# The SSD pipeline of a decoder layer: carried state multiplied by unscaled C on the full array, skip term by a diagonal on the tensor engine, sample state turned

## What is computed

```python
def step(h, inp):                       # once per chunk, h is the carried state
    xc, dtc, Bc, Cc = inp
    acs = jnp.cumsum(dtc * Ar, axis=1)
    decay = jnp.exp(jnp.where(tril, acs[:, :, None] - acs[:, None, :], -jnp.inf))
    xdt = xc * dtc[..., None]
    cb = jnp.einsum('blgn,bsgn->blsg', Cc, Bc)
    y_diag = jnp.einsum('blsg,blsgr,bsgrp->blgrp', cb, decay, xdt)
    y_off = jnp.einsum('blgn,bgrpn,blgr->blgrp', Cc, h, jnp.exp(acs))
    to_end = jnp.exp(acs[:, -1:] - acs)
    h_new = jnp.exp(acs[:, -1])[..., None, None] * h + jnp.einsum('bsgn,bsgr,bsgrp->bgrpn', Bc, to_end, xdt)
    return h_new, y_diag + y_off
...
y = y + d_skip[:, None] * xs            # then the gate silu(z), a norm per group and a gain
```

## Time and profile before

| | us |
|---|---|
| median of 3 runs | 4075.02 (4072.28 to 4075.45) |
| the profiled execution | 4073.7 |
| its span in the profile | 4071.9 |
| first and last instruction of the stage `sg` | 2017.9 to 2324.2 |
| PE, DVE, ACT, POOL busy over the whole span | 3724.5, 1986.9, 943.4, 358.0 |

### The profile page before, as it was taken

The page is one execution under the profiler, slowest core; times in us unless marked ns, Lnnn a source line. Parts: engine busy times, 40 slices in busy tenths (PEclk is TensorE's granted clock), DMA queues, the critical chain, the costliest instruction groups (busy, mean ns, idle before and its releaser), DMA issues. The chain is left out here.

```text
span 4071.9 us, 48044 instructions
## 1 busy us (share of the span) xinstructions
PE 3724.5 (91%) x18116; PEld 2942.2 (72%) x18116; DVE 1986.9 (49%) x4404; ACT 943.4 (23%) x2079; POOL 358.0 (9%) x372
## 2 busy tenths in 40 slices
PE   5999999998996999999777589789899999999997
PEld 3888888885654888888655456445467888888886
DVE  3444444442123888764299732244441354453544
ACT  2111111112131222221377400156300221111111
POOL 0000000000000000000055411354100000000000
PEclk8999999998998999999888699899989999999999
DMA  4333343215441132222367332200114022222222
GB/s 182 121 124 124 117 153 124 103 66 192 115 110 68 53 104 84 83 84 83 101 221 221 114 108 81 71 16 11 60 49 152 11 93 83 83 94 77 90 83 83
DMA packets 178142, 406.45 MB, mean 100 GB/s; under 512 B 25896, under 2 KB 104952, under 8 KB 156648
## 3 DMA queue, kind: packets, MB, share of 16 engines
q1 hardware_dynamic: 162264, 360.48, 26.6%
q10 hardware_dynamic: 12448, 21.78, 1.5%
q0 software_dynamic: 3200, 21.11, 1.4%
HBM read 335.35 MB, written 68.14 MB: 99 GB/s over the span
## 5 line engine op out<-in xcount | busy, mean ns | idle before, releaser
L659 ACT ACTIVATE f_u<-f_Y 128x258 f32<-128x258 f32 x408 | 157.2, 385 | 1093.1 <-PE f_Y L558 1093.1
L785 DVE TENSOR_TENSOR f_g<-f_u,f_Z 128x258 f32<-128x258 f32 x136 | 57.6, 424 | 390.7 <-PE f_Z L558 390.7
L1114 PE MATMUL ps_pp<-h,ps_w 128*128 128x344 f32 x720 | 219.0, 461 | 19.9 <-DMA ps_w<-in_w_att 19.9
L1114 PEld LDWEIGHTS ps_pp<-h,ps_w 128*128 128x128 f32 x720 | 136.0, 192 | 100.2 <-DMA ps_w<-in_w_att 20.3
L755 DVE TENSOR_TENSOR f_g<-f_u,f_X 128x258 f32<-128x258 f32 x136 | 57.6, 423 | 299.3 <-PE f_X L558 293.4
L558 PE MATMUL f_Y<-h,raw 128*128 128x258 f32 x704 | 171.2, 387 | 13.6 <-PEq L111 13.6
L558 PE MATMUL f_Y<-f_a,raw 128*128 128x258 f32 x704 | 170.9, 384 | 6.2 <-issue 6.2
L558 PE MATMUL f_Y<-f_tc,f_sums 128*128 128x258 f32 x704 | 167.5, 380 | 1.9 <-issue 1.2
L558 PE MATMUL f_Y<-f_a,f_sums 128*128 128x258 f32 x704 | 168.8, 380 | 0.0
L558 PE MATMUL f_Y<-f_tc,raw 128*128 128x258 f32 x704 | 167.7, 380 | 0.9 <-ACT f_u L659 0.9
L558 PE MATMUL f_X<-h,raw 128*128 128x258 f32 x704 | 168.1, 382 | 0.0
(11 more groups left out here) (433 smaller groups left out, 7356.5 us busy)
## 6 DMA issues: line engine op xcount, KB each, us to landing
raw<-in_w_f1i SPq DMA_DIRECT2D x44, 1024.0 KB, 4.9
raw<-in_w_f2i SPq DMA_DIRECT2D x44, 1024.0 KB, 4.8
f_wa<-in_w_ada SPq DMA_DIRECT2D x14, 2048.0 KB, 9.7
dn_raw<-in_w_dense SPq DMA_DIRECT2D x28, 1024.0 KB, 5.6
raw<-in_w_f1o SPq DMA_DIRECT2D x16, 1024.0 KB, 4.9
sg_ab<-scr_acs SPq DMA_DIRECT2D x32, 512.0 KB, 5.4
raw<-in_w_f2o SPq DMA_DIRECT2D x16, 1024.0 KB, 4.8
scr_xc<-dn_cv SPq DMA_DIRECT2D x24, 512.0 KB, 4.4
```

The source lines that it names most:

```text
L659: nc.scalar.activation(u[:, i % 2, n], bank[i % 2][:, 0:SUB], ACT.Copy).then_inc(done, 1)
L785: nc.vector.tensor_tensor(g[:, i % 2, 1], u[:, i % 2, 1], Z[i % 2][:, 0:SUB], ALU.add).then_inc(zread, 1)
L1114: m = nc.tensor.matmul(pp[n % 2][:, 0:NC], w[:, t % WR, k], h[:, k, c * NC:(c + 1) * NC], start=k == 0, stop=k == KT - 1)
```

## The change

The carried state's product no longer uses `Cs`. PE multiplies the state `hT` by C as it is, in four products of 128 columns into a new bank `pC`, and DVE multiplies `pC` by exp(acs), which comes from memory as `ea` (written once by `time_steps`). The skip term becomes a product with a diagonal (`dskips`) that accumulates into `pY`. `pY` now has one bank. The triangle mask moves from DVE to POOL, in place in `bt`. The sample state is held with its inner index on partitions: POOL decays it in one operation, PE makes the increment of one sample (`pU`, contraction over eight rows), DVE adds it in one operation, and PE multiplies by C (into `pR`). The norm's factors are spread in two halves and copied to SBUF by ACT (`rb`).

The diff, cut to its core:

```diff
 def through(n):
+    q = n % RS
     pe.wait_ge(copied, UP + n + 1)
     pe.wait_ge(x_w, UP + n + 1)
-    pe.wait_ge(hup, UP + n)
+    pe.wait_ge(hup, UP + n) if n else pe.wait_ge(rows_m, UP + 1 + SG)
     nc.tensor.matmul(pH[:], bt[:, n % 3, 0:P], xw[:, n % 3], start=True, stop=True).then_inc(h_mm, 1)
+    if n % TB:
+        pe.wait_ge(mulled, UP + later(n) - 1)
+        for t in range(GT):
+            m = nc.tensor.matmul(pC[:, t * P:(t + 1) * P], hT[:, (n - 1) % 2, t * P:(t + 1) * P], st[:, q, GT + 1], start=True, stop=True)
+        m.then_inc(c_mm, 1)
+    pe.wait_ge(joined, UP + n)
...
     pe.wait_ge(weighed, UP + n + 1)
...
+        for x in range(2):
+            nc.tensor.matmul(pY[PD * x:PD * (x + 1), t * P:(t + 1) * P], dskips[:, n // TB % 2, t, PD * x:PD * (x + 1)], st[:, q, t],
+                             start=True, stop=False)
+        for x in range(2):
+            r = 2 * t + x
+            m = nc.tensor.matmul(pY[PD * x:PD * (x + 1), t * P:(t + 1) * P], xdt[:, n % 3, r * PD:(r + 1) * PD], E[:, n % 2, r],
+                                 start=False, stop=True)
...
+def grow(m):
+    pe.wait_ge(updated, UP + m)
+    pe.wait_ge(b_masked, UP + m // NB + 1)
+    nc.tensor.matmul(pU[:], bmask[:, m // NB % 2, m % NB], xrow[:, m // NB], start=True, stop=True).then_inc(u_mm, 1)
+
+def read(m):
+    pe.wait_ge(updated, UP + m + 1)
+    for t in range(GT):
+        at = YS + (m // NB * GT + t) * NB + m % NB
+        p = nc.tensor.matmul(pR[:, at:at + 1], H[:, m % RH, t * P:(t + 1) * P],
+                             smc[:, m // NB * XT + GT + 1, m % NB:m % NB + 1], start=True, stop=True)
+    p.then_inc(y_mm, 1)
...
-for i in range(N + 2):
+for i in range(N + LAG + 2):
     if i + 2 < N:
         turn(i + 2)
     if i < N:
         through(i)
-    if i >= 2:
+    if i >= 2 and (i - 2) % TB == 0 and i - 2 <= N:
+        pe.wait_ge(rooted, UP + (i - 2) // TB)
+    if 0 <= i - LAG - 1 < N:
+        read(i - LAG - 1)
+    if 0 <= i - LAG + 1 < N:
+        grow(i - LAG + 1)
+    if 2 <= i < N + 2:
         total(i - 2)
...
 def states(n):
     dve.wait_ge(h_mm, UP + n + 1)
     dve.wait_ge(h_d, UP + later(n))
-    wait_y(dve, n)
+    dve.wait_ge(c_mm, UP + later(n))
...
+def carried(n):
+    k = later(n) - 1
+    dve.wait_ge(c_mm, UP + k + 1)
+    dve.wait_ge(ea_in[k % 2], UP + 32 * (k // 2 + 1))
+    nc.vector.tensor_tensor(y(n), tiles(pC[:]), ea[:, k % 2], ALU.mult).then_inc(mulled, 1)
+
+def join(n):
     wait_y(dve, n + 1)
...
+        nc.vector.tensor_tensor(y(n), y(n), tiles(pY[:]), ALU.add).then_inc(joined, 1)
...
 def update(m):
...
+    dve.wait_ge(decayed, UP + m + 1)
+    dve.wait_ge(u_mm, UP + m + 1)
+    nc.vector.tensor_tensor(H[:, m % RH], H[:, m % RH], pU[:], ALU.add).then_inc(updated, 1)
...
     if i < N:
-        skip(i)
+        if i % TB:
+            carried(i)
+        join(i)
     if i + 1 < N and (i + 1) % TB:
         fade(i + 1)
     if i < N:
         gate(i)
-    if 0 <= i - LAG < UNITS:
+    if 0 <= i - LAG < N:
         update(i - LAG)
-    if 0 <= i - LAG - 1 < UNITS:
-        reduce(i - LAG - 1)
...
 # POOL, per iteration
-    weigh(i + 2)
-    scale(i + 1)
-    read(i - LAG)
+    cut(i + 2)
+    weigh(i + 2)
+    decay(i - LAG + 1)
...
 # time_steps
+sp.dma_start(scr["eacs"].rearrange("(j q) l -> q j l", j=2), grown[:]).then_inc(stored, 16)
+nc.scalar.activation(grown[:], turn[:], ACT.Exp).then_inc(exped, 1)
```

More of the change, by code:

```diff
@@ L2127, in ssd_groups @@
+        rb = ph.sb("rb", [P, TB, P])
         eps = ph.sb("eps", [P, 1])
[L2128 to L2132, removed]
+        H = ph.sb("H", [P, RH, GW])
+        dskips = ph.sb("dskips", [P, 2, GT, P])
+        dab = ph.sb("dab", [P, SH, NB])
@@ L2147, in ssd_groups @@
+        rooted, inv, diagd, spread, kept, scaled, decayed, u_mm, updated, y_mm, small, rows_t, rows_m, skips, b_masked, ssm_saved, ch_s, tail, fallen = (
+            ph.sem(n) for n in ("rooted", "inv", "diagd", "spread", "kept", "scaled", "decayed", "u_mm", "updated", "y_mm", "small", "rows_t",
+                                "rows_m", "skips", "b_masked", "ssm_saved", "ch", "tail", "fallen"))
         block = ph.block()
@@ L2189, in load_state @@
                     sp.wait_ge(H_out[m % RH], UP + 16 * (m // RH))
[L2190 to L2198, removed]
+                    sp.wait_ge(y_mm, UP + m - RH + 1)
+                sp.dma_start(H[:, m % RH], d["state_ssm"][m // NB, m % NB]).then_inc(H_in[m % RH], 16)
             for n in range(2):
@@ L2202, in _ @@
                 sums(n)
[L2203 to L2206, removed]
+            src = bass.AP(scr["steps"].tensor, SH * NB, [[0, P], [1, SH * NB]])
+            sp.dma_start(dab[:].rearrange("p h b -> p (h b)"), src).then_inc(small, 16)
             for n in range(2, RS):
                 chunk(n)
+            growth(1)
             for n in range(RZ):
@@ L2212, in _ @@
                 load_state(m)
[L2213 to L2217, removed]
+            growth(2)
             for i in range(N + LAG + 2):
@@ L2222, in _ @@
                     chunk(i + RS - 1)
+                if 3 <= i + 2 < N and (i + 2) % TB:
+                    growth(i + 2)
                 if RZ <= i + RZ - 1 < N:
@@ L2257, in through @@
+                pe.wait_ge(joined, UP + n)
+                if n % TB == 0:
+                    pe.wait_ge(skips, UP + n // TB + 1)
                 pe.wait_ge(weighed, UP + n + 1)
-                pe.wait_ge(c_s, UP + later(n))
-                pe.wait_ge(skipped, UP + n - 1) if n >= 2 else pe.wait_ge(rows_m, UP + 1)
-                first = n % TB == 0
                 for t in range(GT):
[L2262 to L2269, removed]
+                    for x in range(2):
+                        nc.tensor.matmul(pY[PD * x:PD * (x + 1), t * P:(t + 1) * P], dskips[:, n // TB % 2, t, PD * x:PD * (x + 1)], st[:, q, t],
+                                         start=True, stop=False)
+                    for x in range(2):
+                        r = 2 * t + x
+                        m = nc.tensor.matmul(pY[PD * x:PD * (x + 1), t * P:(t + 1) * P], xdt[:, n % 3, r * PD:(r + 1) * PD], E[:, n % 2, r],
+                                             start=False, stop=True)
+                        if t == GT - 1:
+                            m.then_inc(yd[x], 1)
@@ L2306, in _ @@
             m.then_inc(summed, 1)
-            broadcast(SG - 1)
+            for half in range(2):
+                broadcast(SG - 1, half)
             pe.wait_ge(tail, UP + 3)
@@ L2325, in square @@
                 nc.scalar.activation(sq[:, n % 2], y(n), ACT.Square).then_inc(squared, 1)
[L2327 to L2333, removed]
-                    nc.scalar.activation(H[:, m % RH, b], H[:, m % RH, b], ACT.Identity,
-                                         scale=steps[:, 1, g * GT + t, at:at + 1]).then_inc(decayed, 1)
             def decays(n):
@@ L2352, in roots, with keep @@
                 nc.scalar.activation(root[:, at], pR[:, at], ACT.Sqrt, scale=1.0 / GW, bias=eps[:]).then_inc(rooted, 1)
+            def keep(g, half):
+                act.wait_ge(spread, UP + 2 * g + half + 1)
+                act.wait_ge(scaled, UP + GT * g)
+                nc.scalar.activation(rb[:, 4 * half:4 * half + 4].rearrange("p c l -> p (c l)"), pD[:], ACT.Copy).then_inc(kept, 1)
             decays(0)
@@ L2358, in _ @@
             act.wait_ge(tail, UP + 1)
-            for i in range(N + LAG):
+            for i in range(N + 2):
                 if i + 2 < N:
@@ L2365, in _ @@
                     square(i - 1)
-                if 0 <= i - LAG < UNITS:
-                    decay(i - LAG)
+                if i >= TB + 5 and (i - 5) % TB in (0, 2) and (i - 5) // TB - 1 < SG - 1:
+                    keep((i - 5) // TB - 1, (i - 5) % TB // 2)
                 if i + 2 < N:
                     decays(i + 2)
+            roots(SG - 1)
             for j in range(2):
-                act.wait_ge(reduced, UP + UNITS + 2 + j)
+                act.wait_ge(ch_s, UP + 1 + 2 + j)
                 m = nc.scalar.activation(sqs[:, 2 * j:2 * j + 2].rearrange("p g t b -> p (g t) b"), (h, S)[j][:, :, SEQ:TOK], ACT.Square)
             m.then_inc(tail, 1)
-            roots(SG - 1)
             act.wait_ge(summed, UP + N + 1)
             nc.scalar.activation(root[0:NB, N:N + SG], pR[0:NB, N:N + SG], ACT.Sqrt, scale=1.0 / GW, bias=eps[0:NB]).then_inc(rooted, 1)
+            for half in range(2):
+                keep(SG - 1, half)
         @block.gpsimd
@@ L2456, in update @@
-            def update(m):
-                g, half, t = unit(m)
-                dve.wait_ge(decayed, UP + HB * (m + 1))
-                dve.wait_ge(bc_in[m // GT % 2], UP + 32 * (m // (2 * GT) + 1))
-                for b in range(HB):
-                    at = half * HB + b
-                    v = nc.vector.scalar_tensor_tensor(out=H[:, m % RH, b], in0=bc[:, m // GT % 2, 0, b], scalar=xd[:, g, t, at:at + 1],
```

(2 more changed lines are left out.)

224 lines of the change are left out of this document (121 added, 103 removed).

## The result

| | before | after |
|---|---|---|
| median, us | 4075.23 (4 runs, 4072.28 to 4075.95) | 4203.62 (4 runs, 4201.13 to 4205.77) |
| ratio | | 1.0316, interval 1.0298 to 1.0334 |
| span of the profiled execution, us | 4071.9 | 4201.4 |
| stage `sg`, first to last instruction, us | 306.3 | 440.0 |
| first to last `hT`, 31 chunks, us | 260.5 | 388.4 |

The changed kernel is 3.2% slower; 4176 was forecast, with 4115 to 4230 as the range. The profiled span grew by 129.5 us, and all of that lies in the stage: 133.7 there, less 2.5 that the stage starts earlier and 1.7 behind it.

The account below looks back on a forecast made before the run. The prediction took a closed loop through DVE's and PE's lists as the bound: 31 chunks at 11.6 us, -5 +7, less 260.5, +2 for the ends, gave +103 us; it said 4176 us, range 4115 to 4230.

Parts of the forecast that it names:

- DVE's list is not the measure: Stage `sg`: DVE's list falls from 7.90 to about 5.55 us a chunk, a gain only if DVE never waits.
- The loop closes: Stage `sg`: with one `pU` bank, DVE's and PE's lists run one after the other, 10.3 us a chunk at full clock.
- The rival that ends faster, PE's list as the bound: Stage `sg`: the loop does not close, PE's list sets 7.6 us a chunk; -23 us, 4051; chance 0.06.
- DVE's part and the hand-over: From `pC` through `update` on DVE 5.34 us a chunk, plus 0.12 for the hand-over to PE.
- PE's part at full clock: From `pU` through `pC` on PE 4.81 us a chunk, with `pU` priced like all of `pH`.
- the rival in which their pairs run one after the other: Products into `pY`: pairs with `dskips` and `xdt` run in sequence, 1.7 us more, inside the slow rival; no separate chance.
- The clock: PE in stage `sg`: granted clock stays at 0.82, 36% of the time at half clock, 11.6 us a chunk; chance 0.53.
- rival with the lower clock: PE in stage `sg`: clock falls to 0.66, 13.1 us a chunk; +149 us, 4223; chance 0.17.
- The rival with the full clock: PE in stage `sg`: clock stays full as PE's work rises, 10.3 us a chunk; +63 us, 4137; chance 0.20.
- The sum: Stage `sg`: 31 x 11.6 = 360, -5 +7 = 362, less 260.5 is +101, with the ends +103 us.
- The ends: Outside the 31 chunks: `time_steps` +1 and the tail's norm in two halves +1, together +2 us.
- SP's queue: SP's two more `ea` loads a chunk are issued two chunks ahead and hide.

Follow-up runs that it names:

- e1: The changed kernel with `update(i-2)` as the first operation of DVE's iteration instead of the last; 4075.96 us, 1.0004 of before.
- e2: The changed kernel with PE's product into `pU` for unit i-2 issued between `pC` and `pY`, DVE's order kept; 4068.0 us, 0.9988 of before.
- e5: e2 with SP's row sums issued one chunk earlier and its wait for the growth factors put last in each iteration; 4044.76 us, 0.9930 of before.
- e3: The changed kernel with ten unread products of 128 columns issued by PE ahead of `pU`, loop left closed; 4153.46 us, 1.0195 of before.
- e6: e1 with the new order of SP's queue that e5 has; 4062.63 us, 0.9973 of before.
- e4: The changed kernel with `update` directly after the addition of `pY`, ahead of `hd` and `gate`; 4138.28 us, 1.0163 of before.

## Why the prediction held, step by step

**DVE's list is not the measure.** Right. The work of DVE fell, its operations cost what was taken: `ea`, `pY` and `update` 0.68 to 0.69 us each as durations; from start to start `pY`, `hd` and `gate` took 0.60 or 0.61, but `ea`, priced at 0.59, took 0.81 in the turn shown; `E` 1.52 in the turn shown, where 1.39 and 0.3 for a wait for POOL were taken; `hd` without POOL's `Cs` beside it fell from the 1.81 of the earlier trace rows to a mean of 796 ns (2015 to 2460 us):

```profile
L2472 DVE TENSOR_TENSOR sg_hd<-sg_hT,etot 128x512 f32<-128x512 f32 x28 | 22.3, 796 | 0.0
```

That POOL's product beside it was what made `hd` long is the prediction's estimate from the earlier trace rows; the row agrees with it, but no run here took POOL's work away by itself.

**The loop closes.** Right, and shown from both ends: e1 and e2 open it by moving one operation each and remove 128 and 136 us. The rival that ends faster, PE's list as the bound, needed DVE to be in time; DVE was not, by the 2.5 us of the wait. Once opened, the rival's price came out: 7.6 us a chunk and 4051 were worked out for it, e5 measures 7.23 and 4044.76.

**DVE's part and the hand-over.** Right: 5.46 us were forecast, 5.49 came in the turn shown and 5.3 on average. Within the turn two errors cancel: `E` was 0.17 cheaper than taken, `ea` 0.22 dearer.

**PE's part at full clock.** Right: with 4.81 the loop was 10.3; e3, in which most chunks keep the clock, has 10.16, and from `pU` to the next `hT` a median of 4.82. The choice within it, that `pU` with its eight rows costs as much as `pH` with 128, is shown by the rows: 1.12 us where the clock is full (e3) and 2.07 where it is half, beside 1.02 and 1.91 for `pH`. The products into `pY`, priced at 1.77, take 2160.76 - 2158.87 = 1.89 up to the read in the turn shown; the rival in which their pairs run one after the other, 1.7 more, did not come about.

**The clock.** This is the step that failed, in its size: "a similar share. I keep 0.82, which is 36% of the time at half clock". The clock went to 0.76, half of the time at half clock. But 0.76 in the prediction's own formula gives 1 / (0.52/10.3 + 0.48/15.1) = 12.2 us a chunk, and the loop took 13.0: first to last `hT` less the two first distances, 4.67 and 6.01, in which `update` is not yet part of the loop, is 377.7 for 29 chunks. The rest comes from the formula's second assumption, that the half clock falls evenly on the loop. It does not, as the groups show: it falls on PE's part between `pU` and `pC`. By those groups, taken as the prediction took its pieces, PE's part is 1.30 + 1.60 + 1.53 + 1.62 + 1.24 + 0.2 = 7.5 us (1.53 is the distance from the loads of the transposes to those of `pH` in the turn shown, 2169.61 - 2168.08), and with DVE's 5.46 the loop is 13.0. The prediction had named this in its rival with the lower clock ("the loop's PE part follows the gap and is the part that is slowed"), at 13.1 a chunk and 0.66: its loop time was nearer to the truth than the forecast's, its clock farther.

The rival with the full clock argued from PE's longer list, 7.4 us a chunk in place of 4.6. The list did get longer, and PE's busy share rose from 75 to 81%, yet the clock fell from 0.82 to 0.76. But the share also grows because the same products take longer at half clock (`pH` 1.91 us beside 1.02). Counted in instructions, PE did less per us with the change: 1903 in 370 us (5.1 per us), and 1455 in 247 us (5.9 per us) before. So what failed in that argument is the step from a longer list to a busier PE; whether a PE that does more per us would have had a higher clock is not shown by these rows.

**The chunks in the loop.** A smaller error stood against that one. The sum took 31 chunks at the loop's price, but the first two have no `update` yet and cost 10.7 us together, not 23.2: 12.5 too much. The 29 others took 377.7 us where 29 x 11.6 - 5 + 7 = 338 was forecast for them, 39 too little. That the first error took away part of the second is luck.

**The sum.** From first to last `hT` that leaves 39 - 12.5, or the 388.4 measured less the 362 forecast: +26, which is the whole miss between +103 and the 128.4 of the medians (129.5 in the profiles). The ends were put at +2 and came to 129.5 - 127.9 = +1.6, though not as their terms had it: the stage starts 2.5 us earlier and has its first `hT` 0.6 sooner after that, what lies behind it is 1.7 shorter, and the tail, put at +1, is 31.9 us from the last `hT` to the end in place of 25.5. The spreading of the norm in two halves is not what costs there. From the addition to `sg_ys` to the end it is 13.7 us, and 13.9 before; the 6.7 lie ahead of it, where the two sample units that are still open go through `pU`, `update` and the read one after the other, partly at half clock (eight weight loads take 0.97 us at 2425.51 and 1.83 at 2435.91):

```profile
2427.04 0.68 DVE L2502 TENSOR_TENSOR sg_H<-sg_H,sg_pU 128x512 f32<-128x512 f32 x1
2429.01 0.69 DVE L2502 TENSOR_TENSOR sg_H<-sg_H,sg_pU 128x512 f32<-128x512 f32 x1 [1.28 <-PE sg_pU L2277]
...
2434.42 0.69 DVE L2502 TENSOR_TENSOR sg_H<-sg_H,sg_pU 128x512 f32<-128x512 f32 x1 [1.59 <-PE sg_pU L2277]
...
2441.79 0.29 DVE L2562 TENSOR_TENSOR sg_ys<-sg_pR,sg_sk 128x128 f32<-128x128 f32 x1 [3.09 <-PE sg_pR L2283]
```

**SP's queue.** The prediction let `ea` hide since it is issued two chunks ahead. In the closed loop it does. With the loop open the transfer itself still hides, but the wait in front of it holds back what is queued behind it on SP: that is what e5 took away, 23 us beside e2.

## What to carry to other kernels

A single buffer that passes between two engines makes a loop when its release stands at the end of one engine's list, its wait stands near the head of the other's, and the two lists are tied by a second hand-over. Then the lists add up, and shortening one of them gains its own share and, here, what the clock gives back. Before you count busy time, follow the way from a release to the next wait for it through both lists; if it closes, move the release forward or the wait back, as one moved operation was worth 128 us here. And price the pause that such a wait makes on PE at the work behind it, at the clock that this work gets (here 0.50), not at the mean clock of the stage.

## What was not expected of the hardware

The clock did not follow PE's busy share. Before, PE was busy for 75% of the stage at 0.82; with the change for 81% at 0.76; in e6 for all of the stretch at 0.92; in e5 for 99% at 1.00. The busy share is itself raised by a low clock (`pH` takes 1.91 us at half clock and 1.02 at full clock), so it is a poor sign of how much PE does. What went with the low clock in the closed loop was the pause: 2.5 us at 0.76, 1.2 us at 0.82 (e4), filled at 0.95 (e3, stretch 2053 to 2350 us).

```profile
2053.00:2350.00 297.00, 283.23 (x2358) 232.78 (x2359) 173.12 (x241) 126.56 (x304) 80.91 (x87) 0.95 0.55 176
```

POOL's product for the masked rows of B has eight partitions of 1024 elements, an eighth of the elements of `xw` with its 128 of 512, and took 1.89 us beside 1.04: in this pair the price went with the elements of a partition, not with the number of partitions.

```profile
2157.31 1.04 POOL L2403 TENSOR_TENSOR sg_xw<-sg_xdt,te 128x512 f32<-128x512 f32 x1
2158.31 1.89 POOL L2420 TENSOR_TENSOR sg_bmask<-sg_brow,ident 8x1024 f32<-8x1024 f32 x1
```
